# Setup and convolution of a hybrid decoder step in one program

## The reference, cut to what matters

```
u = rmsnorm(h, g_mix)
a = u @ w_in + b_in                                  # 1024 -> 2048
z = a[..., :1024] * sigmoid(a[..., 1024:])           # the gate
full = concat([ctx, z], axis=1)                      # ctx: 30 rows (prompt: zeros; sample: a cache)
y = depthwise_conv(full, w_dw) + b_dw                # 31 taps per channel
h = h + silu(layernorm(y, ln_g, ln_b)) @ w_out + b_out
new cache rows = full[:, -30:]
```

## Time and profile before

| | us |
|---|---|
| median of 3 runs (range) | 1541.65 (1540.94 to 1546.66) |
| the profiled execution | 1538.84 |
| its span | 1537.0 |
| PE busy / DVE busy / ACT busy / POOL busy | 1164.7 / 483.6 / 291.3 / 53.8 |

### The profile page before, as it was taken

One profiled execution on the slowest core, in us unless ns is written; L12 is line 12 of the kernel. 1 busy time (PEld: TensorE's weight loads), 2 busy tenths in 40 slices (PEclk: granted clock), 3 DMA queues, 4 the chain that ended last, 5 costly groups with the idle time before them and its releaser, 6 DMA issues. The chain is left out here.

```text
span 1537.0 us, 23535 instructions
## 1 busy us (share of the span) xinstructions
PE 1164.7 (76%) x10255; PEld 756.5 (49%) x10255; DVE 483.6 (31%) x1314; ACT 291.3 (19%) x715; POOL 53.8 (4%) x40
## 2 busy tenths in 40 slices
PE   6968997765856765679898897988766685776687
PEld 4846654433533433347665555765443342443356
DVE  2893412112112111224485554142111221212134
ACT  2163231100100110013223431132110110110123
POOL 0340000000000000000000100000000000000000
PEclk9989998878877887899999998899787887787899
DMA  5953289999999999995314342649999999999950
GB/s 153 301 232 141 110 326 422 420 420 420 419 423 418 422 419 377 362 406 188 110 46 148 136 174 110 246 180 418 423 419 420 421 419 422 419 423 416 419 237 29
DMA packets 91569, 477.07 MB, mean 310 GB/s; under 512 B 21964, under 2 KB 33129, under 8 KB 73518
## 3 DMA queue, kind: packets, MB, share of 16 engines
q1 hardware_dynamic: 89060, 455.82, 73.4%
q0 software_dynamic: 1792, 18.88, 3.3%
q10 hardware_dynamic: 602, 0.73, 0.1%
HBM read 473.38 MB, written 2.49 MB: 310 GB/s over the span
## 5 line engine op out<-in xcount | busy, mean ns | idle before, releaser
L926 PE MATMUL ps<-area,hiddenT 128*32 128x256 f32 x2112 | 200.0, 543 | 235.3 <-issue 228.3
L926 PEld LDWEIGHTS ps<-area,hiddenT 128*32 128x32 f32 x2112 | 91.9, 147 | 318.5 <-issue 303.1
L1560 DVE COPY y<-ps 32x256 f32<-32x256 f32 x128 | 53.3, 417 | 476.5 <-PE ps L926 475.7
L916 PE MATMUL ps<-area,uT 128*32 128x256 f32 x2176 | 148.0, 431 | 36.9 <-DMA area<-in_w_exp_up_dram 22.0
L916 PEld LDWEIGHTS ps<-area,uT 128*32 128x32 f32 x2176 | 84.7, 126 | 99.8 <-issue 45.0
L916 PE MATMUL ps<-area,xsT 128*32 128x256 f32 x2048 | 132.7, 415 | 0.0
L1498 ACT COPY y<-ps 32x256 f32<-32x256 f32 x128 | 46.8, 366 | 412.2 <-PE ps L926 411.3
L1230 PE MATMUL ps<-sel,u_rows 128*128 128x256 f32 (+3 forms) x480 | 123.6, 384 | 0.0
L916 PEld LDWEIGHTS ps<-area,xsT 128*32 128x32 f32 x2048 | 80.9, 124 | 53.4 <-issue 22.3
L1609 DVE TENSOR_TENSOR hidden<-silu,ps 128x128 f32<-128x128 f32 x64 | 18.4, 288 | 264.9 <-ACT silu L1514 264.9
L1230 PEld LDWEIGHTS ps<-sel,u_rows 128*128 128x128 f32 (+1 forms) x480 | 75.7, 188 | 40.7 <-issue 31.8
(11 more groups left out here) (348 smaller groups left out, 1264.6 us busy)
## 6 DMA issues: line engine op xcount, KB each, us to landing
area<-in_w_exp_gate_dram SPq DMA_DIRECT2D x66, 2048.0 KB, 26.7
area<-in_w_exp_up_dram SPq DMA_DIRECT2D x66, 2048.0 KB, 30.5
area<-in_w_exp_down_dram SPq DMA_DIRECT2D x66, 2048.0 KB, 26.1
area<-in_conv_w_in_dram SPq DMA_DIRECT2D x8, 1024.0 KB, 11.8
area<-in_w_ple_gate_dram SPq DMA_DIRECT2D x2, 4096.0 KB, 35.2
area<-in_conv_w_out_dram SPq DMA_DIRECT2D x1, 4096.0 KB, 19.3
area<-in_w_o_dram SPq DMA_DIRECT2D x1, 4096.0 KB, 13.3
area<-in_w_uq_dram SPq DMA_DIRECT2D x3, 768.0 KB, 10.5
```

Source lines behind the costliest of these rows:

```text
L916: last = pe.matmul(s.ps[SLOT * j:SLOT * (j + 1), bank, 0:2 * P].rearrange("p (a f) -> p a f", a=2), xT[:, k, :], up[:, :, k, j * P:(j + 1) ...
L926: last = pe.matmul(s.ps[SLOT * g:SLOT * (g + 1), bank, 0:q], hidden[:, SLOT * j:SLOT * (j + 1)], down[:, j, g * q:(g + 1) * q], start=(j = ...
L1560: last = V.tensor_copy(y[a:a + SLOT, (e // PER) % 2, g * q4:(g + 1) * q4], s.ps[SLOT * g:SLOT * (g + 1), 3 + e % 2, 0:q4])
```

## The change

Setup and the first convolution block become one block, and `turn_all`'s work goes into the last block. By part:

- SP loads only the identity (64 KB) before the rows; the remaining constants (620 KB) come behind the first quarter of `w_in`. The gather of the table on ACT has its own semaphore, awaited late.
- PE first runs 20 matmuls of ones by ones, turns vectors and taps, then the rows. Squares are taken chunk by chunk behind the copies.
- Projection m = 0 multiplies `raw` (rows times gain, not yet normalised); DVE multiplies its two results by `rstd` afterwards. m = 1 to 7 take the normalised `s.uT`.
- ACT makes the shifted tap tables by 16 copies, in place of SP's 16 DMAs.
- The gate is one DVE instruction (`gate(m)`), placed within the chain of taps, in place of ACT's linear half and GpSimd's product.
- ACT copies all 12 side groups; PE turns 6 after m = 1 and 6 after m = 2. GpSimd makes the context product.
- Diagonals and copies have four buffers. ACT makes the diagonals of chunks 6 and 7 in 32 small instructions each. PE does chunk 4's taps between m = 6 and m = 7.
- Six of the eight products of the mean are made before chunk 7's taps. The squares are written into `s.uT`. The cache rows are turned behind the squares' sum, copied by ACT behind silu, and stored last.

```diff
+                sp.dma_start(col(s, "ident"), io["constants"][:, 0:P]).then_inc(s.ident_in.sem, 16)
+                (x_prompt, x_sample on setup_in)
+                load_conv_in(sp, s, io, 0)
+                sp.dma_start(s.const[:, P:NCONST], io["constants"][:, P:NCONST]).then_inc(s.const_in.sem, 16)
...
 tensor:
+                for k in range(20):
+                    pe.matmul(s.ps[:, 3, 0:P], s.ones[:], s.ones[:], start=True, stop=True)
+                (turns: vectors, taps; then the rows)
                 norm.sums(pe)
                 for m in range(DC):
                     pe.wait_ge(s.win_in[m // 2].sem, s.win_in[m // 2].at(32))
                     if m >= 2:
-                        pe.wait_ge(s.conv_sig.sem, s.conv_sig.at(m - 1))
+                        pe.wait_ge(s.conv_z.sem, s.conv_z.at(m - 1))
...
+                            done = pe.matmul(s.ps[:, 2 * (m % 2) + half, 0:T], w_in[:, k, a:a + P],
+                                             (s.uT if m else raw)[:, k, :], start=(k == 0), stop=(k == DC - 1))
+                    for k in side_after.get(m, ()):          # {1: range(0, 6), 2: range(6, 12)}
+                        turn(pe, s, g1 + k, side[k][0])
+                    if m == 6:
+                        taps_of(0)
+                for i in range(1, last):
+                    taps_of(i)
+                pe.wait_ge(s.new_columns.sem, s.new_columns.at(1))
+                pe.wait_ge(s.conv_acc.sem, s.conv_acc.at((CW + 1) * len(dve_chunks)))
+                pe.wait_ge(s.conv_evicted.sem, s.conv_evicted.at(2))
+                for c in range(6):
+                    pe.matmul(s.ps[:, 0, 0:T], s.ones[:], acc[:, c, :], start=(c == 0), stop=False)
+                taps_of(last)
 scalar (after the copies, squares and the even chunks of raw):
+                norm.root_on_act(act)
+                for p, q in blocks:
+                    done = nc.scalar.copy(moved[SLOT * p:SLOT * (p + 1), q, :, 0:CW - p],
+                                          s.taps[SLOT * q:SLOT * (q + 1), :, p:CW])
...
+                sigmoid(0); diagonal(2); sigmoid(1); side_copies(1); diagonal(3)
+                sigmoid(2); side_copies(2); sigmoid(3); sigmoid(4)
+                move(0, blocks[0:8]); sigmoid(5); move(0, blocks[8:]); move(1, blocks[0:8])
+                sigmoid(6); move(1, blocks[8:]); move(2, blocks[0:12])
+                sigmoid(7); move(2, blocks[12:]); move(3, blocks[0:8])
+                for i in range(len(pe_chunks)):
+                    evict(i)
+ diagonal(i) on ACT: for q in range(PER): for j in range(STEPS):
+                            done = nc.scalar.activation(diag[:, i, q, j, :], col(s, "fold"), ACT.Copy,
+                                                        scale=moved[:, q, c, PER * j:PER * j + 1])
 gpsimd:
-                for m in range(DC):
-                    G_.tensor_tensor(z[:, m, CTX:CTX + T], lin[:, m % 2, :], sig[:, m % 2, :], ALU.mult)
+                G_.tensor_tensor(ctx4, ctx4, s.taps[:, :, 0:CTX]...broadcast_to([P, DC, NB, CTX]), ALU.mult)
 vector (after its copies, squares, the odd chunks of raw and norm.apply):
+                dve.wait_ge(s.taps_moved.sem, s.taps_moved.at(1))
+                for i in range(2):
+                    diagonal(i)
+                dve.wait_ge(s.conv_mm.sem, s.conv_mm.at(1))
+                V.tensor_tensor(sig[:, 0, :], s.ps[:, 1, 0:T], s.rstd[:], ALU.mult)
+                V.tensor_tensor(lin, s.ps[:, 0, 0:T], s.rstd[:], ALU.mult)
+                gate(0)
+                gates_at = {(0, 18): 1, (1, 14): 2, (2, 0): 3, (2, 16): 4, (3, 0): 5, (3, 16): 6}
+                (the taps of chunks 0 to 3 as before, with these gates before the (chunk, tap) named)
-                (context product, context sum, diagonals 2 and 3)
+                (context sum) ; gate(7) ; (copies for chunk 7, sample columns)
+ gate(m): V.scalar_tensor_tensor(out=z[:, m, CTX:CTX + T], in0=PSUM half, scalar=b_in, in1=sig[:, m % 2, :],
+                                 op0=ALU.add, op1=ALU.mult)
```

More of the change, by code:

```diff
@@ L345, in early_rows @@
     return s.w_ple[0:120, 8:10, :], p_rows.rearrange("p (l i d) -> p l i d", l=2, i=3)
[L348 to L409, removed]
@@ L503, in conv_stage @@
[L503 to L509, removed]
+        sig = room[:, 0:2 * T].rearrange("p (a t) -> p a t", a=2)
+        lin = room[:, 2 * T:3 * T]
+        a, n = 3 * T, 4 * PER * STEPS * SLOT
@@ L514, in conv_stage @@
+        diag = room[:, a:a + n].rearrange("p (n q j m) -> p n q j m", n=4, q=PER, m=SLOT)
+        a += n
+        copies_of = room[:, a:a + 4 * PER * SHIFT].rearrange("p (n q t) -> p n q t", n=4, q=PER)
+        raw = acc
+        squares = z[:, :, CTX:CTX + T]
+        norm = rms_norm(nc, s, s.hT, s.uT, VEC["g_mix"], squares)
         dve_chunks, pe_chunks = [0, 1, 2, 3], [4, 5, 6, 7]
+        last = len(pe_chunks) - 1
         blocks = [(p, q) for p in range(PER) for q in range(PER)]
-        ctx_rows, pin = early_rows(s)
@@ L519, in conv_stage @@
-        g0, groups = s.groups, []
-        for c in range(DC):
-            groups.append(([(ctx_rows[:, i, c * P:(c + 1) * P], 120 * i) for i in range(2)],
-                           [(ctxT[:, c, :], cols_of(P, NB * CTX))]))
+        first = [([(vec_rows[:, 0, :], 0), (vec_rows[0:NVEC - P, 1, :], P)], [(s.vec[:], cols_of(P, NVEC))])]
+        for half in range(2):
+            first.append(([(tap_rows[:, (4 * half + c) * P:(4 * half + c + 1) * P], c * CW) for c in range(4)],
+                          [(s.taps[:, 4 * half:4 * half + 4, :].rearrange("p c k -> p (c k)"),
+                            cols_of(P, 4 * CW))]))
@@ L527, in conv_stage, with gain @@
-        s.groups += len(groups)
+                side.append(([(pin[0:n, i, j, k * P:(k + 1) * P], t0) for j, (t0, n) in enumerate(TILES)],
+                             [(s.pT[:, i, k, :], cols_of(P, T))]))
+        g0, g1 = s.groups, s.groups + len(first)
+        s.groups += len(first) + len(side)
+        side_after = {1: range(0, 6), 2: range(6, len(side))}
+        def gain(c):
+            return s.vec[:, VEC["g_mix"] + c:VEC["g_mix"] + c + 1]
         with nc.Block() as block:
@@ L574, in _ @@
                             if m == 0 and half == 0:
+                                own = (s.raw_act, s.raw_dve)[k % 2]
+                                pe.wait_ge(own.sem, own.at(k // 2 + 1))
+                            if m == 1 and half == 0:
                                 pe.wait_ge(s.normed.sem, norm.ready(k))
-                            last = pe.matmul(s.ps[:, 2 * (m % 2) + half, 0:T], w_in[:, k, a:a + P], s.uT[:, k, :],
-                                             start=(k == 0), stop=(k == DC - 1))
@@ L622, in _ @@
-                    if m == 1:
-                        for k, (_, copies) in enumerate(groups):
-                            if (g0 + k) % 2 == 1:
-                                turned_copy(nc, act, s, g0 + k, copies)
-                    if m > pe_chunks[0]:
-                        move(m - 1 - pe_chunks[0], blocks)
-                move(len(pe_chunks) - 1, blocks[0:8])
-                for i, c in enumerate(pe_chunks):
+                    nc.scalar.activation(sig[:, m % 2, :], src, ACT.Sigmoid, bias=s.vec[:, b:b + 1])\
+                        .then_inc(s.conv_sig.sem, 1)
@@ new lines, in _ @@
+                load(vec_rows[:, 0, :], io["vectors"][0:P])
+                load(vec_rows[0:NVEC - P, 1, :], io["vectors"][P:NVEC])
+                load(tap_rows, io["conv_w_dw"][0])
+                a = VEC["g_ffn"]
+                with nc.allow_non_contiguous_dma(reason="a small table"):
+                    act.dma_start(s.gain[:], io["vectors"][a:a + 2 * DC].rearrange("(l r) q -> l (r q)", l=2)
+                                  .rearrange("l (p c) -> p l c", c=DC)).then_inc(s.gain_in.sem, 16)
@@ new lines, in _ @@
+                for k in range(1, len(first), 2):
+                    turned_copy(nc, act, s, g0 + k, first[k][1])
+                    if k >= x0:
+                        c = k - x0
+                        act.wait_ge(s.turned_out_act.sem, (g0 + k + 1) // 2)
+                        nc.scalar.activation(squares[:, c, :], s.hT[:, c, :], ACT.Square).then_inc(s.squares_act.sem, 1)
+                act.wait_ge(s.turned_out_dve.sem, 1)
+                for c in range(0, DC, 2):
+                    nc.scalar.activation(raw[:, c, :], s.hT[:, c, :], ACT.Copy, scale=gain(c)).then_inc(s.raw_act.sem, 1)
@@ new lines, in _ @@
+                sigmoid(0)
+                diagonal(2)
+                sigmoid(1)
+                side_copies(1)
+                diagonal(3)
+                sigmoid(2)
+                side_copies(2)
+                sigmoid(3)
+                sigmoid(4)
+                move(0, blocks[0:8])
+                sigmoid(5)
+                move(0, blocks[8:]).then_inc(s.conv_moved_act.sem, 1)
+                move(1, blocks[0:8])
+                sigmoid(6)
+                move(1, blocks[8:]).then_inc(s.conv_moved_act.sem, 1)
```

(2 more changed lines are left out.)

274 lines of the change are left out of this document (158 added, 116 removed).

## The result

The changed kernel takes 1533.44 us (median of 5, 1533.03 to 1535.21) against 1542.94 (median of 5), ratio 0.9943 (95%: 0.9925 to 0.9961): 9.5 us faster. The forecast was 1519.5, range 1512 to 1529. Direction right, size less than half. The mark (the end of the mean) is the better measure: 125.10 before, 114.56 + 1.13 = 115.69 after, 9.4 us earlier; forecast 103.2.

What follows compares the result with a forecast made beforehand. Bound: a serial lead-in, then PE waiting for DVE's diagonal before the mean. Gains of 19.1 us after the last projection and 9.8 before the first, less 7.0 between, give 21.9: 1519.5 us, range 1512 to 1529.

Steps and rivals of the forecast that it cites:

- the lead-in: Start of the block to projection 0: rows land near 8.7, squares' sum ends 18.4, projection 0 starts 18.5, before 28.27.
- The warm-up's length: PE's 20 opening matmuls of ones, 40 instructions: 6.1 to 11.0 us, taken as 8.6, ending at 9.5.
- the cold rival: Warm-up does not release the clock before the squares' sum, ending at 25.5; 7 us of gain lost, 1526.5; chance 0.15.
- Side wait: After projections 0 and 1, PE waits for ACT's copy behind diagonal 2: 5.4 us with turns; m = 2 starts 38.1.
- Raw rows: Projection 0 on rows not yet normalised no longer waits for root, reciprocal and norm; it starts at 18.5.
- 9.8 us won: Gain before the first projection, which starts at 18.5 instead of 28.27; one term of the 21.9 us total.
- Front of the taps: From squares' sum to DVE's taps: ACT's tap tables end 25.4, DVE's taps start 29.9 against 50.05, 20 us earlier.
- The product's own length: GpSimd's context product of 1920 elements, run beside DVE's taps: 4.4 to 5.4 us.
- DVE's stall: GpSimd's context product and the two router products hold up DVE's taps, together 5 us.
- The rival of a starved product: GpSimd's context product takes 72.7 us beside the taps, so the mean starts at 128; 1552 us; chance 0.03.
- The end of the block: From the last projection's end (87.5) to the mean's end (103.2): 15.7 us, against 34.8 before.
- the shift of all later work: Work after the mean keeps its lengths and DMA is idle before it, so everything shifts by the 21.9 us gained.

## Why the prediction was wrong

**The step that failed** is in the lead-in: "the rows land near 8.7 ... PE reaches the rows about when they land. Vectors and taps cost 1.1". The sum gave their turns a price and their landing none. Before the change PE used them at 17.0, behind the rows, so no row showed a wait for them. The change put them first, and made their landing (14.58) the one that sets the start. It was to be seen: ACT's queue still moved 4 packets per us at 12 to 14 in the old trace. From 12 to 13 us:

```profile
q10 hardware_dynamic: 4, 0.02, 5.7%
```

With that one DMA split and nothing else changed, the mark is within 0.3 us of the forecast. That it is so close is in part luck. The sum came 1.1 us before its forecast (17.3 against 18.4) and the way from there to the mark took 1.4 us more than forecast (86.2 against 84.8); and of the five profiles with two DMAs and no fillers only this one and the one with 26 products (18.0) kept the clock in the turns, the other three had the sum at 20.3 to 20.9. Turning the taps behind the rows, as the kernel before does, was not tried.

**The clock** came with it. The warm-up's length was 7.0 (range 6.1 to 11.0), but it is lost when a stand follows. Of the 9.8 us some 5 are the landing past 9.5 (14.58) and some 5 the slow turns and sum (13.7 in place of 8.9); the cold rival (25.5) had the mechanism of the second half, for another reason. That the level can fall in the turns was not in the forecast: it fell in the profiles where PE had stood 0.78 to 1.94 us, or 0.76 behind 50 products, and held where it had stood 0.36 or not at all. That the stand is the cause is suggested by the run with 26 products and not shown: it has a shorter stand and a longer warm-up at once.

**Side wait.** The forecast had it (PE stands for ACT behind diagonal 2) and its length (5.4 with turns, 6.1 measured), but not that the clock falls there: 2.8 us on projection 2, 1.9 in the run that otherwise met the forecast.

**Raw rows.** "9.8 us won" took 3.0 of it from here. By the two runs without them, raw rows are worth nothing or less. With them ACT's tap tables and DVE's diagonals set gate 0, not PE, so it comes only 0.4 us earlier, and PE stands 4.23 us for ACT in place of 1.38; behind the longer stand projection 2 lost 2.6 us to the clock (1.7 with two DMAs). The sum should have taken the later of the two chains.

**Front of the taps.** 16 tables 6.38 (forecast 6.4), diagonals 2.77, 32 small products 6.88 (7.0). Missed: the sigmoid's table load, 1.28, runs only when the wait for DVE is over, so DVE's taps began 12.5 us behind the sum in place of 11.5.

```profile
38.29 1.28 ACT L593 ACT_TABLE_LOAD   x1 [3.24 <-DVE area L711]
```

**GpSimd.** The product's own length was forecast 4.4 to 5.4 and is 3.92 where it starts at a gap; DVE's stall was 3.6 by it and 0.4 by a router product, together 4.0 (forecast 5). The mechanism held in each profile: the product got in at a chunk's end (66.24 in the changed kernel), at a chunk's start (54.43, above) or, without raw rows, behind a gate (59.99), and one DVE instruction then took 3.3 to 3.7 us more. The rival of a starved product put its turning point at an end of 109; with its own 14.5 us from the product's end to the mark it is 110.6, which changes nothing.

**The end of the block** (15.6 against 15.7) and the shift of all later work (next load 9.4 us earlier, 168.39 to 159.00; median 9.5) were right. Between the two profiled executions 1.7 us are lost by 199, where the routing ran at clocks of 0.84 and 0.85, and some 4 more later; since the medians keep the whole 9.5, I take it for the spread of single executions. This was not tried.

## What to carry to other kernels

When a consumer is moved ahead of others, ask of each input when it lands, not only what using it costs: a load that nobody waited for has no wait in the trace, and its queue's packets are where to look. Give a DMA an outer dimension that spreads; 31 rows in one piece cost 12 us here; 16 + 15 rows cost nothing in the best profile, and in the others a stand of 0.4 to 1.9 us, mostly with some 3 us of slower turns and sum behind it. And before pricing a shortened chain, follow the other engine's chain to the same point: raw rows saved PE 3 us and cost the end up to 2; early side copies saved it 7 and gave 2.

## What the runs showed of the hardware that I had not expected

- A DMA of 31 rows moved 16 KB per us, 6.0% of sixteen engines' time; placed ahead of the rows in one queue it held them up too, from 9.3 or less to 14.63.
- A stand of 0.8 to 1.9 us ahead of the turns came with a fall to 0.50 within them, though PE is shown as busy throughout; ones products between the turns (0.5 us more for each) did not prevent it behind a stand of 1.94. A stand of 3.03 us ahead of projection 0 came with a fall in two profiles and without one in three.
- GpSimd's product of 1920 columns held DVE for 3.3 to 3.7 us in one piece: in five profiles an addition of two tensors (4.04 in place of 0.42 in the changed kernel), in the three with side copies first and the product on GpSimd a tap with one tensor input (4.07 in place of 0.35 in the first of them), in the three without raw rows a tap with two (3.75 in place of 0.48). I had expected it to cost DVE only where two tensors are read.
